# Out products of two branches moved among and behind the attention's heads, in pairs of columns

## What is computed

```python
xn = rms_norm(h, norm1_g)
u, v, q, c_kv, q_idx, k_idx, w_idx, gates = split(xn @ w_in)
y_a = chunked_spatial_gating(u, v, ...)            # first branch, width 512
y_b = dsa_attention(qh, k, vv, qi, ki, wi)         # second branch, 4 heads of 128, softmax over chosen keys
g = sigmoid(gates.reshape(bsz, s, 2, d))
merged = g[:, :, 0] * (y_a @ w_a_out) + g[:, :, 1] * (y_b @ w_b_out)
h = h + merged @ w_o
hn = rms_norm(h, norm2_g)
h = h + peer(hn, ...)   # per token 8 heads x 16 experts: 128 rows of u_tab and 128 of v_tab (4 KB each) are fetched
```

## Time and profile before

| | us |
|---|---|
| three runs, median (lowest to highest) | 1689.75 (1686.3 to 1693.33) |
| the profiled execution | 1679.32 |
| its span in the trace | 1677.6 |
| items 4 to 7 of the attention begin on DVE at | 904.43 |
| the last of 8 `wo` columns is read by DVE at | 979.95 |
| the first gather of the expert layer is issued at | 997.59 |

### The profile page before, as it was taken

The page is one execution under the profiler, slowest core; times in us unless marked ns, Lnnn a source line. Parts: engine busy times, 40 slices in busy tenths (PEclk is TensorE's granted clock), DMA queues, the critical chain, the costliest instruction groups (busy, mean ns, idle before and its releaser), DMA issues.

```text
span 1677.6 us, 19908 instructions
## 1 busy us (share of the span) xinstructions
PE 1473.7 (88%) x7335; PEld 1094.4 (65%) x7335; DVE 1134.2 (68%) x2257; ACT 621.4 (37%) x1361; POOL 380.2 (23%) x382
## 2 busy tenths in 40 slices
PE   6999999999899899999978898878787778977777
PEld 6788888889787799998968797333333333422222
DVE  6866875558855866677777578786767768454444
ACT  2322122225546544453443464333333334222222
POOL 2000110012000100010000223544344435634440
PEclk9999999999999999998989999989898989999999
DMA  9554585446532355553322657999999999999998
GB/s 371 194 170 144 192 278 176 152 144 187 189 102 63 126 194 181 164 189 123 125 71 63 207 179 294 422 421 421 421 417 393 382 392 398 423 422 421 422 421 337
DMA packets 87632, 435.85 MB, mean 260 GB/s; under 512 B 9776, under 2 KB 14000, under 8 KB 54512
## 3 DMA queue, kind: packets, MB, share of 16 engines
q0 software_dynamic: 45024, 298.08, 44.3%
q1 hardware_dynamic: 42512, 136.50, 24.6%
...
## 4 chain that ended last, share of the span: by engine, by line
PE 57%; DVE 22%; DMA 12%; ACT 6%; issue 2%; POOL 0%; SPq 0%; ACTq 0%; DVEq 0%; POOLq 0%
PE ps L516 14%; PE ps L517 14%; PE ps L518 14%; DMA WF<-in_puv,AB 11%; PE ps L836 11%; DVE WR L1208 3%; DVE WF L2014 1%; ACT WR L856 1%; ACT L1183 1%; DVE ring L2014 1%; DMA ring<-in_w_adaT 1%; DVE HF L2014 1%; DVE work L1266 1%; DVE AF L1951 1%; DVE AF L1946 1%
## 5 line engine op out<-in xcount | busy, mean ns | idle before, releaser
L516 PE MATMUL ps<-HR,WR 128*128 128x256 f32 (+1 forms) x1240 | 396.3, 320 | 13.1 <-DVE WR L1208 9.9
L1208 DVE TENSOR_TENSOR WR<-ring,WR 128x1024 fp32r<-128x1024 f32 (+2 forms) x254 | 286.8, 1137 | 159.0 <-ACT WR L856 158.4
L517 PE MATMUL ps<-HR,WR 128*128 128x256 f32 (+1 forms) x1240 | 390.4, 315 | 0.0
L518 PE MATMUL ps<-HR,WR 128*128 128x256 f32 (+1 forms) x1240 | 390.0, 315 | 0.0
L856 ACT CAST WR<-ring 128x1024 fp32r<-128x1024 f32 (+2 forms) x254 | 242.8, 964 | 329.9 <-PE ps L518 329.8
L516 PEld LDWEIGHTS ps<-HR,WR 128*128 128x128 f32 x1240 | 238.8, 193 | 32.3 <-issue 13.7
L517 PEld LDWEIGHTS ps<-HR,WR 128*128 128x128 f32 x1240 | 238.6, 192 | 14.8 <-issue 0.8
L518 PEld LDWEIGHTS ps<-HR,WR 128*128 128x128 f32 x1240 | 238.4, 192 | 13.8
L516 PE MATMUL ps<-AR,WR 128*128 128x256 f32 (+2 forms) x519 | 161.7, 312 | 6.9 <-POOL AR L2077 4.8
L836 PE MATMUL ps<-ring,AB 128*128 128x512 f32 x256 | 126.1, 636 | 41.0 <-ACT AB L1193 41.0
L517 PE MATMUL ps<-AR,WR 128*128 128x256 f32 (+2 forms) x519 | 160.7, 310 | 0.0
...
## 6 DMA issues: line engine op xcount, KB each, us to landing
...
```

The lines of the kernel that those rows point to most:

```text
L516: e.matmul(o, l[0], r[0], start=first, stop=False)
L517: e.matmul(o, l[0], r[1], start=False, stop=False)
L518: return e.matmul(o, l[1], r[0], start=False, stop=last)
L1208: e.tensor_tensor(WS[:, m % NSP, 1, 0:nk * cols], ring[:, (NA + m) % NS, 0:nk * cols], WS[:, m % NSP, 0, 0:nk * cols].bitcast(F32), ALU.su ...
```

## The change

1. Weights of `wa` and `wb` are stored in pairs of columns: 4 tiles of 1024 for each instead of 8 of 512. `out_pair` makes two columns (24 matmuls) into one bank. The matmuls are the same in number and size.
2. The four `wa` pairs enter `SEC` as fillers behind g15, and so fall between the last `pv2` and `back2` steps; the four `wb` pairs follow at the list's end.
3. The gating is done on 512 columns at once (`gate_wa`, in place in `sgx`; `gate_wb`, into `F`), DVE adds the two branches itself (into `F`), ACT rounds 512 columns (`high_merged`), POOL subtracts for pairs 0 to 2, DVE for pair 3. POOL adds nothing any more.
4. `wo` 0 and 1 are begun with k 0 to 5 both, and closed with k 6 and 7.
5. In the attention, DVE's reciprocal and division of item n-1 stand behind the maximum of item n (that of item 7 in the step of `back2` 6).
6. SP's load of the sub-keys waits for the merged pair 3 instead of the last `wb` gating.

```diff
@@ -160,7 +160,7 @@
     fillers += [("proj", "vA", j) for j in range(4)] + [("proj", "u", j) for j in range(4)]
-    fillers += [("proj", "g", j) for j in range(16)]
+    fillers += [("proj", "g", j) for j in range(16)] + [("proj", "wa", j) for j in range(4)]
@@ -193,7 +193,7 @@
         fill()
-    return out + fillers
+    return out + fillers + [("proj", "wb", j) for j in range(4)]
@@ -462,12 +462,10 @@
             if s[0] == "proj":
-                tile(T["w2"][base2[s[1]] + s[2]], 8, 128, s[1], s[2])
+                src = T[s[1]][s[2]] if s[1] in ("wa", "wb") else T["w2"][base2[s[1]] + s[2]]
+                tile(src, 8, 128, s[1], s[2])
             elif s[0] == "wi":
                 tile(T["w2w"], 8, 4, "wi")
-        for d in range(8):
-            tile(T["wa"][d], 4, 128, "wa", d)
-            tile(T["wb"][d], 4, 128, "wb", d)
         for d in range(8):
@@ -693,10 +691,29 @@
+            def out_pair(w, c, rhs, ready):
+                o = bank(w, c)
+                m = last_tile(w, c)
+                q.wait_ge(s_lo, m + 1)
+                wh, wl = halves(m)
+                for d in range(2):
+                    for k in range(4):
+                        q.wait_ge(*ready(k))
+                        x = three(o[:, 256 * d:256 * d + 256], (wh[:, 4 * d + k, :], wl[:, 4 * d + k, :]), rhs[k],
+                                  d == k == 0, d == 1 and k == 3)
+                x.then_inc(*mm.to("w", m))
+                mm.also(w, c)
+
+            def merged(c):
+                return dv.at("mg", c) if c == 3 else po.at("mg", c)
+
             for s in SEC:
...
                         natural(s[1:], 2, dv.at("sec", "h", 7))
+                    elif s[1] in ("wa", "wb"):
+                        out_pair(s[1], s[2], ya_p if s[1] == "wa" else yb_p,
+                                 (lambda k: dv.at("ya", 1)) if s[1] == "wa" else (lambda k: dv.at("yb", k)))
                     elif s[1] in UNSCALED:
@@ -781,11 +798,20 @@
                     x.then_inc(*mm.to("z", c))
-            for d in range(8):
-                project(("wa", d), ya_p, 256, lambda k: dv.at("ya", 1))
-                project(("wb", d), yb_p, 256, lambda k: dv.at("yb", k))
-            for d in range(8):
-                project(("wo", d), [(mgp[:, 0, k, :], mgp[:, 1, k, :]) for k in range(8)], 256, lambda k: po.at("mg", k))
+            for ks in (range(0, 6), range(6, 8)):
+                for d in range(2):
+                    m = last_tile("wo", d)
+                    o = (bank("wo", d) if ks[0] == 0 else bank_of("wo", d))[:, 0:256]
+                    q.wait_ge(s_lo, m + 1)
+                    wh, wl = halves(m)
+                    for k in ks:
+                        q.wait_ge(*merged(k // 2))
+                        x = three(o, (wh[:, k, :], wl[:, k, :]), (mgp[:, 0, k, :], mgp[:, 1, k, :]), k == 0, k == 7)
+                    if ks[0]:
+                        x.then_inc(*mm.to("w", m))
+                        mm.also("wo", d)
+            for d in range(2, 8):
+                project(("wo", d), [(mgp[:, 0, k, :], mgp[:, 1, k, :]) for k in range(8)], 256, lambda k: merged(k // 2))
@@ -1060,12 +1086,20 @@
             root(("f2",), R(3, 4))
+
+            def high_merged(c):
+                q.wait_ge(*dv.at("merged", c))
+                e.copy(mgp[:, 0, 2 * c:2 * c + 2, :], F[:, c % 3, :].rearrange("p (j t) -> p j t", j=2)).then_inc(
+                    *ac.to("mg hi", c))
+
             for s in SEC:
...
                     o = bank_of(w, j)[:, 0:256]
-                    if w in UNSCALED:
+                    if w == "wb" and j:
+                        high_merged(j - 1)
+                    if w in UNSCALED + ("wa", "wb"):
                         continue
@@ -1124,10 +1158,7 @@
                     e.activation(s_[:, 4:5], s_[:, 3:4], ACT.Sqrt).then_inc(*ac.to("vroot", s[1]))
-            for d in range(8):
-                hi_for("wb", d)
-                q.wait_ge(*po.at("merged", d))
-                e.copy(mgp[:, 0, d, :], F[:, d % 3, 0:256]).then_inc(*ac.to("mg hi", d))
+            high_merged(3)
             for d in range(8):
@@ -1830,9 +1861,31 @@
+            def gate_wa(c):
+                q.wait_ge(*ac.at("ps", "g", 2 * c + 1))
+                q.wait_ge(*mm.at("wa", c))
+                x_ = sgx[:, 2 * c:2 * c + 2, :]
+                e.scalar_tensor_tensor(out=x_, in0=x_, scalar=1.0, in1=two(bank_of("wa", c)[:, :]), op0=ALU.add,
+                                       op1=ALU.mult).then_inc(*dv.to("ps", "wa", c))
+
+            def gate_wb(c):
+                f = two(F[:, c % 3, :])
+                if c == 3:
+                    q.wait_ge(*po.at("mg", 0))
+                q.wait_ge(*ac.at("ps", "g", 15))
+                q.wait_ge(*mm.at("wb", c))
+                e.scalar_tensor_tensor(out=f, in0=g1[:, 2 * c:2 * c + 2, :], scalar=1.0, in1=two(bank_of("wb", c)[:, :]),
+                                       op0=ALU.add, op1=ALU.mult).then_inc(*dv.to("ps", "wb", c))
+                q.wait_ge(*dv.now())
+                e.tensor_tensor(f, f, sgx[:, 2 * c:2 * c + 2, :], ALU.add).then_inc(*dv.to("merged", c))
+
             for s in SEC:
                 if s[0] == "proj":
+                    if s[1] == "wb":
+                        gate_wa(3) if s[2] == 0 else gate_wb(s[2] - 1)
                     lo_for(s[1], s[2])
+                    if s[1] == "wa" and s[2]:
+                        gate_wa(s[2] - 1)
                     if s[1] in ("ki", "ck"):
@@ -1890,8 +1943,12 @@
                     row_max(n, P2[:, n % 4, :], 1.0, "2")
-                    q.wait_ge(*ac.at("exp2", n))
-                    row_scale(n, P2[:, n % 4, :], "2")
+                    if n:
+                        q.wait_ge(*ac.at("exp2", n - 1))
+                        row_scale(n - 1, P2[:, (n - 1) % 4, :], "2")
+                elif s[0] == "back2" and s[1] == 6:
+                    q.wait_ge(*ac.at("exp2", 7))
+                    row_scale(7, P2[:, 3, :], "2")
                 elif s[0] == "pv2":
@@ -1899,19 +1956,10 @@
                     gated(s[1], s[2])
-            for d in range(8):
-                f = d % 3
-                lo_for("wa", d)
-                lo_for("wb", d)
-                if d >= 3:
-                    q.wait_ge(*po.at("mg", d - 3))
-                q.wait_ge(*ac.at("ps", "g", 8 + d))
-                q.wait_ge(*mm.at("wa", d))
-                e.scalar_tensor_tensor(out=F[:, f, 0:256], in0=sgx[:, d, :], scalar=1.0, in1=bank_of("wa", d)[:, 0:256],
-                                       op0=ALU.add, op1=ALU.mult).then_inc(*dv.to("ps", "wa", d))
-                q.wait_ge(*mm.at("wb", d))
-                e.scalar_tensor_tensor(out=F[:, f, 256:512], in0=g1[:, d, :], scalar=1.0, in1=bank_of("wb", d)[:, 0:256],
-                                       op0=ALU.add, op1=ALU.mult).then_inc(*dv.to("ps", "wb", d))
+            gate_wb(3)
+            q.wait_ge(*ac.at("mg hi", 3))
+            e.tensor_tensor(mgp[:, 1, 6:8, :], two(F[:, 0, :]), mgp[:, 0, 6:8, :].bitcast(F32), ALU.subtract).then_inc(
+                *dv.to("mg", 3))
@@ -2068,14 +2116,10 @@
                 *po.to("causal"))
-            for d in range(8):
-                f = d % 3
-                q.wait_ge(*dv.at("ps", "wb", d))
-                e.tensor_tensor(F[:, f, 0:256], F[:, f, 0:256], F[:, f, 256:512], ALU.add).then_inc(*po.to("merged", d))
-                q.wait_ge(*po.now())
-                q.wait_ge(*ac.at("mg hi", d))
-                e.tensor_tensor(mgp[:, 1, d, :], F[:, f, 0:256], mgp[:, 0, d, :].bitcast(F32), ALU.subtract).then_inc(
-                    *po.to("mg", d))
+            for c in range(3):
+                q.wait_ge(*ac.at("mg hi", c))
+                e.tensor_tensor(mgp[:, 1, 2 * c:2 * c + 2, :], F[:, c, :].rearrange("p (j t) -> p j t", j=2),
+                                mgp[:, 0, 2 * c:2 * c + 2, :].bitcast(F32), ALU.subtract).then_inc(*po.to("mg", c))
             add_squares("wo", 7, sq(0, 1), lambda k: sq(1 + (k - 1) % 3, 2 + (k - 1) % 3))
@@ -2127,7 +2171,7 @@
                 if m == first_wq + 1:
-                    q.wait_ge(*dv.at("ps", "wb", 7))
+                    q.wait_ge(*dv.at("merged", 3))
                     e.dma_start(skw, T["sk"]).then_inc(s_k, 16)
@@ -2270,7 +2314,7 @@
         "wuk": tiles(i["w_uk_2"][0]), "wuv": tiles(i["w_uv_2"][0]),
-        "wa": tiles(i["w_a_out_2"][0]), "wb": tiles(i["w_b_out_2"][0]), "wo": tiles(i["w_o_2"][0]),
+        "wa": pairs(i["w_a_out_2"][0]), "wb": pairs(i["w_b_out_2"][0]), "wo": tiles(i["w_o_2"][0]),
         "wq": tiles(i["peer_wq_2"][0]),
```

## The result

| | us |
|---|---|
| after, four runs, median (lowest to highest) | 1665.91 (1660.89 to 1669.59) |
| before beside it, four runs | 1688.03 (1682.31 to 1693.33) |
| ratio, 95% interval | 0.9872, 0.9843 to 0.9901 |
| after, the profiled execution (span) | 1666.53 (1664.8) |

The kernel became faster by 1.28%, some 22 us with an interval of 17 to 27. I had forecast 1674.5 with a range from 1667 to 1684: the sign was right and the gain was sized too small.

What follows compares the result with a forecast made beforehand. DMA-bound gathers would simply start earlier: `wa` at 915.3 plus 49.4 us of PE work puts the eighth `wo` column at 964.7 against 979.95, 15.2 us earlier. From 1689.75 that gives 1674.5 us, range 1667 to 1684.

Steps and rivals of the forecast that it cites:

- The start of the gathers sets the end: Expert layer: its duration stays at 680 us from first gather to end, so only an earlier start gains time.
- The step of items 4 to 7: Attention's last items on DVE: double-width tiles lengthen each step from 3.12 to 4.07 us, a price of 1.5 us.
- From the first `wa` matmul to the eighth `wo` column: Dense stretch of projections: PE is the bound and takes 49.4 us, with the eighth column read at 964.7.
- Cover: Merge pair 2: ready at 942.2, before `wo` 0 asks for it at 942.9, a margin of 0.7 us.
- The front: Attention items before item 4: late division fills two DVE waits of 0.67 us, so item 4 begins 1.3 us earlier.
- The clock: g15 and `pv2` 0 on PE: possible half clock after waits; first `wa` matmul put at 915.3, between 914.2 and 916.6.
- the ring of DVE and ACT: Items 4 to 7: chain of mask, maximum, exponential, copy, high part and low part across both engines, 4.07 us a step.
- the local bounds: Gain at the eighth `wo` column: between 12.1 and 17.7 us, around the expected 15.2.
- own range: Whole kernel: time between 1672 and 1677.7 us, before widening for the scatter of runs and other cases.
- Half clock in `wa`: Interleaved `wa` tiles: PE stays at half clock, costing 8.6 us, leaving a gain of 6.6, time 1683.1; chance 0.10.
- taken back: Expert layer: its loop over DVE, ACT and PE sets the end and cancels the gain, time 1689.75; chance 0.06.
- slower: `wa`, `wb` and `wo`: half clock holds throughout, costing 34.6 us against the 15.2 gained, time 1709; chance 0.04.
- The case of more gain: All front waits count and the clock never falls, or `wo` 0 and 1 gain: 18 to 20 us, 1670 to 1672; chance 0.04.

Runs made afterwards that it cites:

- late division alone: The kernel before with only each item's reciprocal and division moved behind the next item's maximum; median 1681.3 us, ratio 0.9961.
- after again: The changed kernel run once more, unedited, with a second trace (also called the repeat of after); median 1665.11 us, ratio 0.9878.
- division early: The changed kernel with each division put back behind its own item's exponential; median 1670.04 us, ratio 0.99.
- `wa` behind: The changed kernel with the four `wa` pairs behind the attention instead of among its last steps; median 1669.99 us, ratio 0.9896.
- high part first: The changed kernel with ACT making the next tile's high part ahead of the exponential in items 4 to 7; median 1662.89 us, ratio 0.9894.
- both: The changed kernel with ACT's high part ahead of the exponential in items 4 to 7 and item 3 divided in its own step; median 1661.96 us, ratio 0.9891.
- both, turn behind: The changed kernel with high parts ahead of exponentials, item 3 divided in its step, and projections before turns from item 4; median 1658.67 us, ratio 0.9846.

## Why the prediction was wrong

**What held.** The start of the gathers sets the end: 679.0 to 680.8 us from first gather to end in the traces of before and after, and 678.0 to 683.0 in all. The step of items 4 to 7 is 4.07 us in after (907.56 to 919.79 is three steps of 4.08), as worked out. From the first `wa` matmul to the eighth `wo` column it is 968.11 - 918.51 = 49.6, against 49.4. Pair 2 of the merge is ready at 945.90 (POOL's third subtraction, 944.34 and 1.56 long); `wo` 0 starts at 944.87 and asks for it twelve matmuls later, at 946.31. Cover 0.4 us where I had 0.7. Closing `wo` 0 and 1 late is worth about 1 us, as the kernel without it shows.

**The front.** This term failed first. I let two of four waits of 0.67 us count and took 1.3 us. Measured from the mark item 4 gained 2.9 in one trace of after, 3.3 in the other and 3.3 with the late division alone. That is more than even my upper bound, 2.7 for four waits. The mark's count for items 0, 1, 2 and 3 says why: before 9.32, 17.58, 25.13, 30.63; after 9.63, 16.66, 23.45, 28.51. Every interval shrank: 1.2, 0.8, 0.4 and, to item 4, 0.8 us. The first is about 0.67 plus the reciprocal and division themselves, 0.5 us (861.13 to 861.60 on DVE before): they had stood ahead of work for which PE waited. In the trace of before that wait is plain to see, and I hadn't looked there. Timeline of PE, before:

```profile
871.90 4.05 PE L781 MATMUL ps<-AB,AF 128*128 128x128 f32 x16 [4.14 <-DVE AF L1819]
```

After, the two rows that answer to it wait 1.41 and 0.28 us, and the turn ahead of them 0.56, where before it didn't wait: 2.25 instead of 4.14 in all. I had taken the items 0 to 3 for covered by projections, and had read only item 3. 1.6 to 2.0 us are missing in the sum here.

**The clock.** I added 1.1 us for a clock at half in g15 and `pv2` 0. In one trace of after the clock stayed at 1.00 through a wait of 3.41 us. In the other it fell, and cost 0.1 to 0.2 us (60.63 against 60.55 to the eighth `wo` column, 11.15 against 10.95 to the first `wa` matmul), because the ring of DVE and ACT was the longer one there. So the term should have been next to nothing either way. PE's loss had been added on top of steps that I had myself made 4.07 us long, and of which PE's work fills 3.56. The fall was also shorter than priced: 1.5 us in g14's step, where full half clock up to `pv2` 0 would have been 2.4. From item 4 to the first `wa` matmul it took 10.95 us, against 12.2 forecast and 11.1 without the term.

These two and two tenths of smaller ones are the whole of the local difference: 15.2 + 1.6 + 1.25 - 0.2 = 17.85.

**The level.** The rest I can't trace to a mechanism. The forecast stood on 1689.75, the median of three runs; with a fourth it was 1688.03, and fifteen, ten and seven runs of before on later occasions gave 1686.99, 1683.2 and 1685.17. So 1.7 of the 8.6 us by which I missed 1665.91 are the level, 2.65 the terms above, and 4.2 are left over between 17.85 at the mark and 22.1 between the medians. I don't assign these. With both terms right the sum would have given 17.85 and, from 1688.03, 1670.2, which lies inside the range: that the time fell 1.1 below it rests on these 4.2, whose cause stays open. The three executions of before that were traced took 1679.32, 1681.1 and 1683.23, all faster than its median of fifteen, so no trace shows a typical one. The interval, 16.7 to 26.5, holds 17.85, and over the timed kernels the two measures differ to both sides, though the ratio gives more in five of these seven:

| kernel | gain at the first gather, us | gain by the ratio (interval) |
|---|---|---|
| after again | 18.2 | 20.6 (16.2 to 25.1) |
| late division alone | 5.7 | 6.6 (3.5 to 9.6) |
| division early | 13.8 | 16.9 (11.6 to 22.3) |
| `wa` behind | 15.4 | 17.5 (13.3 to 21.6) |
| high part first | 18.1 | 17.8 (12.3 to 23.2) |
| both | 20.4 | 18.3 (11.1 to 25.6) |
| both, turn behind | 23.1 | 26.0 (20.1 to 31.7) |

All seven local gains lie inside their intervals. The range was too narrow: the local bounds alone reached to 17.7, which the gain passed, and below the own range of 1672 I left 5 us for the scatter of the runs and for more gain together.

**The rivals.** Half clock in `wa` fell: the windows from 916 on are at 1.00 in both traces of after. So did "taken back" and "slower". The case of more gain, 18 to 20 us for front and clock, to which I gave 0.04, came nearest: 17.85 and 18.2 in the traces, though its 1670 to 1672 also lies above the time. The Trainium skill (TensorE: Matmul & The Clock Gate, "HAM oscillation — how this bites in real kernels") describes a kernel whose long waits between bursts throw the array back to half rate each time. The traces agree in part, since a wait of 3.40 us did so in the repeat of after and one of 3.41 us didn't in the first. That every item's gap would count by it was my reading; the section speaks of waits longer than the bursts. In before the clock fell all the same around shorter ones, 1.41, 1.87 and 1.76 us, to 0.79 and 0.50 in the windows from 912 to 920.

The Trainium skill (SBUF — State Buffer, "Who interferes with whom") has a VectorE instruction with two SBUF inputs contend with a GpSimd instruction that reads SBUF; I had weighed that at 0.5 us late for pair 2. Here the trace agrees with the mechanism and not with my price: with DVE's low part, POOL's subtraction overlaps by 0.4 us (943.52 + 1.22 against 944.34) and takes 1.56 instead of 1.26 to 1.29, and the cover of 0.4 us is left. In the kernel in which POOL adds as well the overlaps are larger, 0.94 to 1.13 us, and there the longer chain of POOL, these overlaps and the clock together cost 5.7 us.
